# Residual adds of two mid-network norms moved from VectorE to GpSimd, with one up tile and two token chunks issued behind the norms

## What is computed

```python
def first_block(x, ...):
    ...
        h = h + rmsnorm(z @ w_out[l], mix_norm_post[l])
        u = rmsnorm(h, ffn_norm_pre[l])
        gt = causal_dwconv(u @ ffn_w_gate[l], ffn_conv_w[l], ffn_conv_b[l])
        y = (jax.nn.gelu(gt, approximate=True) * (u @ ffn_w_up[l])) @ ffn_w_down[l]
        h = h + rmsnorm(y, ffn_norm_post[l])
    return h[:, N_META:]

def rmsnorm(x, gain):
    xf = x.astype(jnp.float32)
    y = xf * lax.rsqrt(jnp.mean(xf * xf, axis=-1, keepdims=True) + EPS)
    return (y * gain.astype(jnp.float32)).astype(x.dtype)
```

## Time and profile before

| what | us |
|---|---|
| median of 3 runs | 2985.7 |
| lowest and highest run | 2985.19, 2990.61 |
| profiled execution, its time | 2990.51 |
| its span, first to last instruction | 2988.8 |
| mean granted TensorE clock, share of full | 0.96 |
| TensorE busy in the span | 2765.5 |
| VectorE busy | 1679.1 |
| ScalarE busy | 1184.9 |
| GpSimd busy | 511.9 |
| norm of the FFN, first scale to first matmul of tile 1 | 789.5 to 840.1 |
| norm of the second projection, first scale to tile 0 | 1571.6 to 1631.9 |

### The profile page before, as it was taken

How to read it: one execution, slowest core, us unless ns; L and a number is a source line. 1 busy time by engine, 2 the same in 40 slices (tenths; PEclk the granted TensorE clock), 3 DMA queues, 4 the chain that set the end, 5 groups by cost and what they waited for, 6 DMA issues and landing times. The chain is left out here.

```text
span 2988.8 us, 38390 instructions
## 1 busy us (share of the span) xinstructions
PE 2765.5 (93%) x14590; PEld 2416.9 (81%) x14590; DVE 1679.1 (56%) x2113; ACT 1184.9 (40%) x1714; POOL 511.9 (17%) x299
## 2 busy tenths in 40 slices
PE   9989999898899999999998998998999499999993
PEld 7989999798789999988777888666776388888883
DVE  5356655361434334333334832664444699999996
ACT  4342333321321111122334213554433377777774
POOL 3000000002122212200110000002610134444441
PEclk9999999999999999999999999999999699999996
DMA  5342322343121111113313121113302399999996
GB/s 193 101 129 92 97 87 90 119 125 123 67 64 48 43 49 49 47 44 105 141 63 106 43 64 57 37 49 92 106 24 113 139 405 417 416 417 414 414 413 242
DMA packets 244298, 436.92 MB, mean 146 GB/s; under 512 B 21698, under 2 KB 180690, under 8 KB 218594
## 3 DMA queue, kind: packets, MB, share of 16 engines
q1 hardware_dynamic: 234690, 400.88, 37.2%
q0 software_dynamic: 9504, 34.61, 2.9%
HBM read 375.54 MB, written 59.90 MB: 146 GB/s over the span
## 5 line engine op out<-in xcount | busy, mean ns | idle before, releaser
L3456 DVE TENSOR_TENSOR k_w_lo<-k_raw,k_w_hi 128x2048 fp32r<-128x2048 f32 x192 | 433.4, 2289 | 41.0 <-ACT k_w_hi L3392 37.3
L3392 ACT CAST k_w_hi<-k_raw 128x2048 fp32r<-128x2048 f32 x192 | 363.0, 1912 | 67.0 <-PE bank L3312 41.2
L120 PE MATMUL bank<-u_ffn_hi,f_w_hi 128*128 128x342 f32 (+1 forms) x840 | 292.1, 348 | 5.6 <-POOL f_w_lo L1329 5.6
L122 PE MATMUL bank<-u_ffn_hi,f_w_lo 128*128 128x342 f32 (+1 forms) x840 | 293.0, 349 | 0.0
L121 PE MATMUL bank<-u_ffn_lo,f_w_hi 128*128 128x342 f32 (+1 forms) x840 | 292.8, 349 | 0.0
L120 PE MATMUL bank<-u_hi,p_w_hi 128*128 128x342 f32 (+2 forms) x720 | 237.7, 330 | 8.9 <-DVEq L878 6.0
L122 PE MATMUL bank<-u_hi,p_w_lo 128*128 128x342 f32 (+2 forms) x720 | 231.8, 322 | 0.0
L121 PE MATMUL bank<-u_lo,p_w_hi 128*128 128x342 f32 (+2 forms) x720 | 231.7, 322 | 0.0
L3310 PE MATMUL bank<-k_w_hi,k_x_hi 128*128 128x512 f32 x512 | 203.8, 398 | 5.4 <-DVE k_x_lo L3462 5.1
L3312 PE MATMUL bank<-k_w_hi,k_x_lo 128*128 128x512 f32 x512 | 200.5, 392 | 0.0
L3311 PE MATMUL bank<-k_w_lo,k_x_hi 128*128 128x512 f32 x512 | 200.3, 391 | 0.0
(11 more groups left out here) (566 smaller groups left out, 6753.5 us busy)
## 6 DMA issues: line engine op xcount, KB each, us to landing
k_raw<-in_w_e_gate_dram SPq DMA_DIRECT2D x64, 1024.0 KB, 7.1
k_raw<-in_w_e_up_dram SPq DMA_DIRECT2D x64, 1024.0 KB, 7.7
k_raw<-in_w_e_down_dram SPq DMA_DIRECT2D x64, 1024.0 KB, 8.2
d_raw<-in_ffn_w_down_dram SPq DMA_DIRECT2D x44, 512.0 KB, 3.3
p_w<-in_w_in_dram SPq DMA_DIRECT2D x34, 512.0 KB, 4.3
f_raw<-in_ffn_w_gate_dram SPq DMA_DIRECT2D x22, 512.0 KB, 3.7
f_raw<-in_ffn_w_up_dram SPq DMA_DIRECT2D x22, 512.0 KB, 3.7
gate_scratch<-g_out SPq DMA_DIRECT2D x20, 513.0 KB, 6.4
```

The lines of the kernel that those rows point to most:

```text
L120: pe.matmul(out, wh[:, t, :], xh[t][:, c:c + n], start=t == 0, stop=False)
L122: m = pe.matmul(out, wl[:, t, :], xh[t][:, c:c + n], start=False, stop=t == tiles - 1)
L3392: act.copy(wh[:, q, :], raw[:, r, :]).then_inc(hi_made, 1)
L3456: dve.tensor_tensor(wl[:, q, :], raw[:, r, :], wh[:, q, :], ALU.subtract).then_inc(lo_made, 1)
```

## The change

The eight residual adds of each norm go from VectorE's program to the head of GpSimd's, each waiting for its scale. VectorE's program loses them, and the low part of a tile is now made two steps behind its scale instead of one. In the FFN the first up tile is no longer taken step by step; it is a whole product behind the eight steps. In the second projection four chunks are taken in the steps, and chunks 4 and 5 behind them, ahead of the turn of the root. The high parts of tiles 0 and 1 there wait only for as many parts of group 0's memory as they overwrite, and stand ahead of the last chunk's keeping; VectorE makes the two low parts ahead of the gates' biases.

```diff
         @block.gpsimd
         def _(pool):
+            for k in range(KD):
+                pool.wait_ge(scaled, k + 1)
+                pool.tensor_tensor(h[:, k, :], h[:, k, :], y[:, k, :], ALU.add).then_inc(h_made, 1)
             pool.wait_ge(first_lo, 2)
             pool.sem_inc(lo_g, 2)
             pool.sem_inc(lo_u, 2)
...
-            pe.wait_ge(lo_g, 2)
-            pe.wait_ge(lo_u, 2)
+            pe.wait_ge(first_lo, 2)
...
                 pe.wait_ge(u_lo, k + 1)
-                first(0, LIVES, 0, 0, k, gmm)
-                first(1, SEQS, 3, TAPS - 1, k, umm)
+                first(k)
+            for j, (c, w) in enumerate(SEQS):
+                m = product(pe, bank[3 + j][:, 0:w], (wh[:, 1], wl[:, 1]), u, TAPS - 1 + c, w)
+            m.then_inc(umm, 1)
             pe.wait_ge(logs2, len(LIVES))
...
-    EARLY = 6
+    EARLY, BEHIND = 4, 6
...
         @block.gpsimd
         def _(pool):
+            for k in range(KD):
+                pool.wait_ge(scaled, k + 1)
+                pool.tensor_tensor(h[:, k, :], h[:, k, :], y[k], ALU.add).then_inc(h_made, 1)
...
             m.then_inc(gmm, EARLY)
+            wide(0, EARLY, BEHIND)
             pe.wait_ge(logs2, len(SEQS))
             pe.wait_ge(rstd2, len(SEQS))
...
             m.then_inc(turned2, 1)
-            wide(0, EARLY)
+            wide(0, BEHIND)
...
                 if n < 2:
-                    act.wait_ge(gmm, NB)
+                    act.wait_ge(g_used, -(-(n + 1) * D // WIDTHS2[0]))
...
-            for c in range(NB):
+            for c in range(NB - 1):
                 keep_group(0, c)
             high(0)
             high(1)
+            keep_group(0, NB - 1)
...
+            low(0)
+            low(1)
             dve.wait_ge(sig_made, NB)
             dve.tensor_tensor(gt[:, :, :], gt[:, :, :], gb[:, :].unsqueeze(1).to_broadcast([P, NB, 2 * ML_H]), ALU.add).then_inc(gates_made, 1)
-            low(0)
-            low(1)
```

More of the change, by code:

```diff
@@ L1345, in tile, with first @@
                 m.then_inc(umm, 1)
[L1347 to L1352, removed]
+            def first(k):
+                for j, (c, w) in enumerate(LIVES):
+                    out, cols = bank[j][:, 0:w], slice(c, c + w)
+                    pe.matmul(out, wh[:, 0, k, :], uh[k][:, cols], start=k == 0, stop=False)
+                    pe.matmul(out, wh[:, 0, k, :], ul[k][:, cols], start=False, stop=False)
+                    m = pe.matmul(out, wl[:, 0, k, :], uh[k][:, cols], start=False, stop=k == KD - 1)
                 if k == KD - 1:
-                    m.then_inc(done, 1)
+                    m.then_inc(gmm, 1)
             pe.sem_inc(umm, 2)
-            pe.wait_ge(lo_g, 2)
-            pe.wait_ge(lo_u, 2)
+            pe.wait_ge(first_lo, 2)
             pe.wait_ge(logs, len(LIVES))
@@ L1444, in tile @@
                 m.then_inc(inner_made, 1)
-            def add(k):
-                dve.wait_ge(scaled, k + 1)
-                dve.tensor_tensor(h[:, k, :], h[:, k, :], y[:, k, :], ALU.add).then_inc(h_made, 1)
             dve.wait_ge(rstd_made, len(LIVES))
             scale(0)
-            add(0)
             for e in range(2):
@@ L1453, in _ @@
                 dve.tensor_tensor(wl[:, e, :, :], raw[:, e, :, :], wh[:, e, :, :], ALU.subtract).then_inc(first_lo, 1)
-            for k in range(1, KD):
+            scale(1)
+            for k in range(2, KD):
                 scale(k)
-                if k == 1:
-                    low(0)
-                add(k)
-                if k > 1:
-                    low(k - 1)
+                low(k - 2)
+            low(KD - 2)
             low(KD - 1)
@@ L1714, in _, with wide @@
         def _(pe):
-            def wide(n, first=0):
+            def wide(n, first=0, end=NB):
                 h, l = group(wh, n), group(wl, n)
-                for c in range(first, NB):
+                for c in range(first, end):
                     i = NB * n + c
@@ L1875, in scale @@
                 dve.scalar_tensor_tensor(y[k], y[k], gain[k], rstd, ALU.mult, ALU.mult).then_inc(scaled, 1)
-            def add(k):
-                dve.wait_ge(scaled, k + 1)
-                dve.tensor_tensor(h[:, k, :], h[:, k, :], y[k], ALU.add).then_inc(h_made, 1)
             def low_stream(k):
@@ L1939, in _ @@
             scale(0)
-            add(0)
             low_group(0, 0)
-            for k in range(1, KD):
+            scale(1)
+            low_group(0, 1)
+            for k in range(2, KD):
                 scale(k)
-                if k == 1:
-                    low_stream(0)
-                add(k)
                 low_group(0, k)
-                if k > 1:
-                    low_stream(k - 1)
+                low_stream(k - 2)
+            low_stream(KD - 2)
             low_stream(KD - 1)
```

## The result

The changed kernel takes 2996.78 us (median of five runs, 2992.27 to 3000.24) against 2985.7. Ratio 1.0036, 95% interval 1.0024 to 1.0047: slower, by about 11 us. The profiled execution took 3000.24 us, with a span of 2998.3 against 2988.8.

The account below looks back on a forecast made before the run. TensorE, busy 93% of the span, was taken as the full engine; the FFN's +0.1 and the second projection's +8.0 sum to +8.1 us, which on 2985.7 gives 2994 us, range 2984 to 3000.

Parts of the forecast that it names:

- First come, first served, in turns: Both norms: VectorE's passes and GpSimd's adds never run at once; whichever arrives first goes first, then they alternate.
- The hold: Both norms: time one GpSimd add keeps VectorE out, taken as 2.20 us, counting 8 times in each part.
- my step: Second projection's norm: VectorE/GpSimd step of 5.2 us, including 0.13 when the add finds the way free and starts afresh.
- The FFN, +0.1 forecast: FFN's norm: loop at almost the old pace, up product fills the wait behind it; sum +0.1 us.
- the walk: FFN's norm, reckoned pass by pass: first low part ready at 800.9, TensorE's loop ending 831.3, up product 842.4.
- The second projection, +8.0 forecast: Second projection's norm: loop +4.8, two chunks behind it bringing +8.6, possible clock gain -0.4, wait and half clock -5.0; +8.0 us.
- -5.0: Behind the second projection's norm: the wait of 3.27 us ahead of tile 0 and the half clock behind it go.
- -0.4: Behind the second projection's loop: gain if the 1.7 us lost to the clock in 1616.3 to 1628.6 does not recur; at most 0.8.
- A: Both norms: adds run beside VectorE, TensorE binds both loops; together -8.2 us, 2978, faster; chance 0.12.
- B: Both norms: exclusive, but shorter holds or less left over at the ends; +0 to +6, about 2990; chance 0.24.
- C: Both loops: TensorE falls to half clock between steps and becomes the late one; 12 us more, 3006; chance 0.06.
- The row that I held against C: Over 1880 to 1950: TensorE said to wait at every step, busy 64 of 70 us, keeping clock 0.96.

Follow-up runs that it names:

- +9.8 with the second: The changed kernel, unchanged, compared once more with the kernel before: 2994.35 us beside 2984.51, ratio 1.0030.
- order_only: Changed kernel with the adds back on VectorE and its old program and order in both norms, against the kernel before: 2979.16 us beside 2986.72, ratio 0.9979.
- read_beside: order_only plus eight GpSimd additions in the FFN on memory nobody uses: ratio 1.0037 to the kernel before, FFN 13.8 us longer than order_only.
- ffn_part: The kernel before with only the FFN part of the change: 2986.66 us beside 2986.72, ratio 1.0002.
- half_behind: order_only, but half the up tile stays in the FFN's steps and five chunks in the projection's; against the kernel before: 2976.20 us beside 2985.54, ratio 0.9966.
- tail_only: The kernel before with only the second projection's reordering behind its norm, adds and chunks as before: 2981.27 us beside 2985.54, ratio 0.9984.

## Why the prediction was right, point by point

**The sum.** Forecast +8.1 and 2994; measured +11.1 with the first comparison (2996.8) and +9.8 with the second. In the profile the two places themselves lost +0.4 and +8.1, 8.5 together. The difference to the 9.6 of the span is the +2.0 around 1790 less the 0.9 given back elsewhere; the spread of whole runs is wider than what is left.

**The resource.** That adds and passes exclude each other was taken from two places of the trace of before. It is shown: by the steps of the changed kernel, by order_only as the counterpart, and by read_beside without any dependence. "First come, first served, in turns" held in these norms, but not as a rule: at 2103.13 of the same trace an instruction of GpSimd waited for four passes. The hold was taken as 2.20 and is 2.27 where the add had to queue (FFN), 2.37 where it started free (projection, with the 0.13 of restart in my step: 2.33). The steps came out at 4.55 for 4.48, and 5.27 for 5.2 (adds at 1591.03 and 1596.32, 5.29).

**The FFN, +0.1 forecast, +0.4 measured.** Loop end 831.32 (831.3 by the walk), tile 1 at 842.24 (842.4). The granted clock behind it is 1.00 over 842 to 862, where the earlier trace rows have 0.89. These absolute times flatter the walk, since the changed kernel's first scale came 0.33 earlier (789.19). From the first scale, the first low part was ready after 11.40 us (800.59, as 797.22 and 3.37; 11.4 by the walk), five steps were 0.05 to 0.07 longer each, and tile 1 came after 53.05 us where I had 52.9: +0.3 against before. The last 0.1 wasn't traced.

**The second projection, +8.0 forecast, +8.1 measured.** By its terms, each kernel counted from its own first scale: loop end after 49.56 us (1620.92) against 44.81 (1616.36), +4.75 (forecast +4.8). The two chunks 1620.92 to 1629.59, 8.67 (8.6). From the turn to tile 0 12.20 us instead of 15.53, and from tile 0 to the first take 11.20 (1641.79 to 1652.99) instead of 12.82 (1631.89 to 1644.71): -3.33 and -1.62, 4.95 together, where I had -5.0 and another -0.4. The -0.4 was the wrong guess: I hoped that the half clock of 1619.3 would not recur, and it did, as the piece from 1632.7 to 1636.1. Up to the first take the terms thus make +8.5, not +8.1. The other 0.4 came back between the last two takes, where ffn_part with its untouched code shows the same; it is in no term of mine. That the total fits to 0.1 is luck; that the loop, the chunks and the tail each came within 0.1 of their terms is not.

**The rivals.** A (2978) needed passes of 1.28 beside the adds: they are 3.4. B (lighter holds) needed holds below 2.2: they are above. C (half clock in the loops) had a share in the projection: there the clock stayed at half over all of 1571.2 to 1588.3, in which TensorE was busy 7.17 of 17.1 us, and ScalarE's square of tile 3 waited 4.95 us for a sum of squares at half clock. It cost nothing that can be seen, since the pair was the later one all the same: the first low part was ready at 1584.76 (1583.49 and 1.27; 1584.8 by my walk), low(5) at 1610.84 (1609.57 and 1.27; 1610.8 by my walk). In the FFN's loop TensorE waited 1.14 us in every step, and the granted clock was 1.00 over 800 to 834. The Trainium skill, "TensorE: Matmul & The Clock Gate", section "HAM oscillation — how this bites in real kernels", tells of a kernel in which long waits bring the half clock back in every group of matmuls; with waits of 1.14 us the trace doesn't show it here. The row that I held against C was weaker than I made it: over 1880 to 1950 TensorE had six waits of 0.8 to 1.2 us, at three places 22 us apart and not in every step, and the 0.96 are half-clock pieces at both ends of the window (up to 1882.9 and from 1947).

**What the prediction lacked.** The +2.0 between 1733 and 1824. I took the difference to carry over one to one behind tile 0. It did, up to the last take; then TensorE, with the same 23.06 busy microseconds of 25, got a clock of 0.93 where the kernel before had 1.00. The stage has a spot in which TensorE is idle for 1.94 us, in both kernels. The first two rows are of the kernel before, the third of the changed one:

```profile
1760.00:1785.00 25.00, 23.06 (x109) 19.59 (x108) 6.59 (x13) 3.41 (x8) 0.00 (x0) 1.00 0.21 66
1780.30 0.41 PE L1730 MATMUL bank<-i_w_hi,u_mix_hi 128*128 128x384 f32 x1 [1.94 <-DVE i_w_lo L1866]
...
1788.58 0.41 PE L1731 MATMUL bank<-i_w_hi,u_mix_hi 128*128 128x384 f32 x1 [1.94 <-DVE i_w_lo L1869]
```

In the changed kernel the half clock sets in 1 us behind that wait and lasts 3.5 us. That the piece comes from this spot falling at another moment is only argued. What is shown: it is in all three profiles of kernels that hold the change's second part whole (1789.7, 1791.1, 1785.6), and not in those of the eight others (the kernel before, and seven variants that hold the second part in pieces or not at all), which have 88.9 to 89.2 us for that stretch.

## What to carry to other kernels

An instruction moved to GpSimd leaves VectorE's program but not VectorE's time, if it reads SBUF and VectorE's own passes take two operands from SBUF (here a pass with a single one of 0.81 us was held too, while passes with one from SBUF and one from a bank ran free): look in the trace for one place where both meet, and add the *whole* hold to the pair's step. Then judge a reordering and a move of work apart, since here one was worth -8.6 us and the other +8.3, and the sum hid both. Compare the stretches around the edit with a profile in which they are untouched: the projection differed by 1.4 us with no edit in it. When work is taken out of a loop to cover a wait behind it, take out only as much as brings TensorE's step down to the next engine's (3.85 against 3.66 in half_behind's FFN); more than that is idle time in the loop and full price behind it. Where no wait is left to cover, as in the projection once its tail was reordered, work behind the loop only costs.

## What I had not expected of the hardware

- A GpSimd fill of 2.02 us ran beside two VectorE passes without delaying either, while an addition of 1.90 us delayed VectorE by 1.64. The duration wasn't what mattered.
- The half clock at the start of the second norm ended 6.8 us behind the first scale in the kernel before and 17 in the changed one, but also 8.7 in tail_only, whose loop is untouched and took 1.06 us longer; ffn_part's projection, untouched too, was 1.4 shorter. That bounds what a single profile can say of a stage.
- A half-clock piece appeared 150 us behind the edit and was there in each of three profiles (2.0 us).
